# Two-layer block on one core: norms in blocks, gated attention outputs, a three-pass output projection, and a quarter of the gate rows on ScalarE

## The chip, the cores and the metric

One core of a Trainium2 chip runs the whole program in one launch. The metric is the device time of one execution in microseconds (us), as the median over runs. The engines are TensorE (PE, with its weight loads shown apart as PEld), VectorE (DVE), ScalarE (ACT), GpSimd (POOL) and SyncE (SP), which issues most DMAs. They run side by side and meet only at semaphores.

## The reference

The input is one sequence of 256 tokens with 1024 features, all in float32. Two layers follow each other. In layer 1, `h` goes through `rms_norm(h, g) * (1 + scale) + shift`, a projection, two mixers (a softmax attention and a recurrent mixer), a gated sum and `w_out`; then through a second norm and an expert layer, which for each token picks 8 x 16 of 16384 experts. In layer 2 the same kind of norm is followed by a projection, two attentions of 8 heads with 128 features (a: with three branches, b: with a compressed latent), and this:

```python
g_a, g_b = jnp.split(jax.nn.sigmoid(bgate), 2, axis=-1)
x = x + gate_a * ((g_a * o_a + g_b * o_b) @ w_o)
# rms_norm, scale and shift again, then a feed-forward with a short convolution:
# up (1024 -> 2 x 2816), conv, silu(gate) * up, down (2816 -> 1024), times gate_f, plus x
```

`scale`, `shift` and the gates of both layers come from one dot product for each feature between a conditioning vector and a row of `w_ada`.

## The kernel before

Everything is held transposed: 1024 features are 8 blocks of 128 partitions, 256 tokens lie along the free axis. The residual `hT` and the normed `xn` are 128x8x256. Weights come as 478 tiles of 128x1024 (512 KB) in one fixed order through `wring`, which has 6 slots; SyncE loads tile n when tile n - 6 is done (`tile_done`). Results go to three banks in turn, and the engine that empties one counts `ring_free`.

Products are made in two ways. Plain fp32 ones (`matmul8`, L438; `matmul8_tokens`, L488) take the weight slot as it is. Split ones (`three`, L463; `split8`, L470) take an upper part of the weight, rounded by ScalarE into one of three `whi` slots (`act_hi`, L450), and a rest that VectorE forms in `wlo` (`tile_lo`, L457), each against an upper and a lower part of x (`xhi`, `xlo`): three products for one. The phases in `SPLIT` are made this way; w_out and w_o are plain.

There is no planner: each engine has its program written out in order, and the order of the calls in the blocks at the end of the file is its queue. The phases that matter here:

- **Start.** VectorE does 16 dot products of `w_ada` (L822), the first norm, then 4 tiles of w_in by tokens (L492).
- **A norm** (four of them) is `norm_squares` (one VectorE operation over all 8 blocks, L514), `norm_pe` (8 products with ones, L506), `norm_act` (Sqrt, L511), `norm_scale` (reciprocal L518, one scaling over all blocks L519), `norm_shift` (8 operations, L523), `x_upper` on ScalarE (L530) and `x_rest` (L536). `pe_w_in` and `pe_w_in2` wait for all 8 blocks of `xn`, `pe_route` and `pe_ffn` for all of `xlo`. The two tiles after the second and fourth norm then need their own `act_hi` and `tile_lo`.
- **w_out** (L1422): VectorE adds each tile to `hT` (`dve_residual`, L1430) and does dot products of `w_ada` beside it (`dve_late_ada`, L1419; `dots_before` says how many by tile).
- **Routing and gate rows.** After the top-16 search on VectorE, the gates of 256 tokens are spread to a 128x128 table each, in 64 groups of 4 tokens: VectorE makes `A4` (one comparison over 512 columns, L1589) and `B4` (four operations of 128 columns, one a token, L1591), TensorE multiplies them (L1606) and does one eighth of an early expert tile (L1496), ScalarE copies the bank into the table `G` (L1616). `A4` and `B4` have two buffers, the banks four. After each eighth group ScalarE has a Gelu (L1505).
- **Expert stage** (256 tiles), then transposes, the residual (L1794) and the third norm.
- **Second attention** (`att_pe`, `att_act`, `att_dve`, `att_pool`, L575 to L687): 24 jobs for attention a and 8 for b, as a software pipeline in turns; in turn t VectorE finds the maxima of job t + 3, the reciprocals of job t + 1 and copies the output bank of job t - 2 (L674). GpSimd scales the probabilities (L686). After the last one VectorE multiplies `oA` and `oB` by their gates and adds them, three operations of 2048 columns (L2091 to L2093), and w_o starts (L2189).
- **Feed-forward** (66 tiles, split), at its end 8 additions into `hT` (L1803) and one store of 1 MB (L2323).

## Time and profile before

| | |
|---|---|
| median of 3 runs | 1910.35 us (1909.63 to 1910.8) |
| profiled execution | 1909.39 us |
| its span, first to last instruction | 1907.6 us |
| mean granted TensorE clock | 0.962 of full |
| busy: PE, PEld, DVE, ACT, POOL | 1731.3, 1503.9, 1337.7, 728.6, 98.9 us |
| HBM read, written | 309.63 MB, 5.51 MB |

Busy times are sums over one profiled execution; engines overlap, so they don't add up to the span. A TensorE that is shown busy may still be below its pace, since matmuls are pipelined and their ends are modelled. A row of a timeline gives the start, the busy time, the engine, the line of the code, the operation, what is written and read, the shape and the count; in brackets stands the idle time before it and what ended it.

### The profile page before, as it was taken

To read this page: it belongs to the slowest core of one execution; us is meant where nothing else is said; L and a number is where in the kernel's file an instruction comes from. 1 tells how busy PE (TensorE), PEld (TensorE's weight loads), DVE (VectorE), ACT (ScalarE), POOL (GpSimd) and SP (SyncE) were. 2 spreads that over 40 slices of the span, in tenths; PEclk is the share of its full clock that TensorE was granted. 3 is DMA by queue.
4 is the path that set the end of the run, shared out by engine and by line. 5 is a ranking of instruction groups with operands and counts; after the bars stand their busy time and mean duration, and the time that the engine had idled before them with its cause. 6 is when DMAs were issued, how large, how long until landed. Compare 5 with 4: busy or idle time off the path is not lost.

```text
span 1907.6 us, 30181 instructions
## 1 busy us (share of the span) xinstructions
PE 1731.3 (91%) x10370; PEld 1503.9 (79%) x10370; DVE 1337.7 (70%) x2720; ACT 728.6 (38%) x1275; POOL 98.9 (5%) x107
## 2 busy tenths in 40 slices
PE   2987999969997989999999999999799988879997
PEld 2986888759885767788888888887798846669997
DVE  7678553763999977688888888887445545448886
ACT  1443101113212344455555555554244215324443
POOL 0022000000000000000000000000007103200000
PEclk8999999989998989999999999999899988989999
DMA  9642003655561127677777777777355460035553
GB/s 332 233 136 69 23 16 108 216 216 165 159 189 46 56 81 242 211 234 240 233 237 235 236 239 234 239 234 222 110 181 152 125 209 1 23 96 180 182 181 110
DMA packets 101311, 316.24 MB, mean 166 GB/s; under 512 B 11248, under 2 KB 20464, under 8 KB 100720
## 3 DMA queue, kind: packets, MB, share of 16 engines
q1 hardware_dynamic: 100512, 311.07, 51.2%
q10 hardware_dynamic: 720, 4.11, 0.6%
q8 instruction: 50, 0.82, 0.2%
q14 instruction: 29, 0.24, 0.0%
HBM read 309.63 MB, written 5.51 MB: 165 GB/s over the span
## 4 chain that ended last, share of the span: by engine, by line
PE 77%; DVE 17%; DMA 2%; issue 2%; POOL 1%; ACT 1%; SPq 0%; ACTq 0%; DVEq 0%; POOLq 0%
PE bank L481 8%; PE bank L466 7%; PE bank L467 7%; PE bank L468 7%; PE bank L1647 6%; PE bank L1649 6%; PE bank L1651 6%; PE bank L482 4%; PE bank L1606 4%; PE bank L442 3%; PE bank L492 2%; PE bank L1398 2%; PE bank L582 1%; PE bank L1496 1%; PE bank L485 1%
## 5 line engine op out<-in xcount | busy, mean ns | idle before, releaser
L460 DVE TENSOR_TENSOR wlo<-wring,whi 128x1024 fp32r<-128x1024 f32 x348 | 423.9, 1224 | 114.5 <-ACT whi L455 106.7
L455 ACT CAST whi<-wring 128x1024 fp32r<-128x1024 f32 x364 | 380.9, 1048 | 73.5 <-PE bank L1651 49.1
L466 PE MATMUL bank<-xboth,whi 128*128 128x256 f32 x960 | 276.3, 288 | 25.5 <-DVE wlo L460 23.3
L467 PE MATMUL bank<-xboth,whi 128*128 128x256 f32 x960 | 273.3, 285 | 0.0
L468 PE MATMUL bank<-xboth,wlo 128*128 128x256 f32 x960 | 273.2, 285 | 0.0
L481 PE MATMUL bank<-xboth,whi 128*128 128x512 f32 x658 | 235.8, 397 | 0.0
L466 PEld LDWEIGHTS bank<-xboth,whi 128*128 128x128 f32 x960 | 186.0, 194 | 28.9 <-issue 24.4
L467 PEld LDWEIGHTS bank<-xboth,whi 128*128 128x128 f32 x960 | 186.1, 194 | 0.6 <-issue 0.5
L468 PEld LDWEIGHTS bank<-xboth,wlo 128*128 128x128 f32 x960 | 185.9, 194 | 0.0
L482 PE MATMUL bank<-xboth,wlo 128*128 128x256 f32 x658 | 184.5, 280 | 0.0
L1647 PE MATMUL bank<-whi,Whi 128*128 128x512 f32 x512 | 161.0, 396 | 14.9 <-DVE Wlo L1742 14.9
L1649 PE MATMUL bank<-wlo,Whi 128*128 128x512 f32 x512 | 159.9, 394 | 0.0
L1651 PE MATMUL bank<-whi,Wlo 128*128 128x512 f32 x512 | 159.0, 392 | 0.0
L481 PEld LDWEIGHTS bank<-xboth,whi 128*128 128x128 f32 x658 | 123.6, 188 | 29.4
L1496 PE MATMUL bank<-xn,wring 128*128 128x256 f32 x544 | 128.6, 380 | 0.0
L482 PEld LDWEIGHTS bank<-xboth,wlo 128*128 128x128 f32 x658 | 124.2, 189 | 3.7
L1647 PEld LDWEIGHTS bank<-whi,Whi 128*128 128x128 f32 x512 | 97.3, 191 | 33.4 <-issue 9.8
L1649 PEld LDWEIGHTS bank<-wlo,Whi 128*128 128x128 f32 x512 | 97.2, 190 | 21.5
L1651 PEld LDWEIGHTS bank<-whi,Wlo 128*128 128x128 f32 x512 | 97.0, 189 | 21.4
L1496 PEld LDWEIGHTS bank<-xn,wring 128*128 128x128 f32 x544 | 98.6, 191 | 10.7
L1751 DVE TENSOR_TENSOR arena<-arena 128x256 f32<-128x256 f32 x94 | 59.8, 636 | 56.0 <-ACT arena L1710 56.0
L460 POOL TENSOR_TENSOR wlo<-wring,whi 128x1024 fp32r<-128x1024 f32 x16 | 45.7, 2862 | 1016.4 <-ACT whi L455 1016.4
(367 smaller groups left out, 2893.5 us busy)
## 6 DMA issues: line engine op xcount, KB each, us to landing
wring<-in_w SPq DMA_DIRECT2D x463, 512.0 KB, 3.9
arena<-in_ada SPq DMA_DIRECT2D x48, 512.0 KB, 5.6
xn<-in_ada SPq DMA_DIRECT2D x96, 256.0 KB, 3.3
h_spill<-arena SPq DMA_DIRECT2D x34, 128.0 KB, 1.7
arena<-h_spill SPq DMA_DIRECT2D x34, 128.0 KB, 3.5
wring<-in_w SPq DMA_DIRECT2D x6, 384.0 KB, 3.1
wring<-in_w SPq DMA_DIRECT2D x9, 256.0 KB, 2.6
arena<-in_const ACTq DMA_DIRECT2D x1, 1200.0 KB, 5.3
```

Of the source, the lines that this page charges most:

```text
L455: act.copy(whi[:, n % HSLOTS, :], wring[:, n % SLOTS, :]).then_inc(hi_ready, 1)
L460: eng.tensor_tensor(wlo[:, n % SLOTS, :], wring[:, n % SLOTS, :], whi[:, n % HSLOTS, :].bitcast(F32), ALU.subtract).then_inc(lo_ready, 1)
L466: pe.matmul(out, h, xh, start=start, stop=False, **kw)
L467: pe.matmul(out, h, xl, start=False, stop=False, **kw)
L468: return pe.matmul(out, l, xh, start=False, stop=stop, **kw)
L481: pe.matmul(out, h, xboth[:, k, :, :], start=(k == 0), stop=False)
L482: pe.matmul(out[:, 0:S], l, xhi[:, k, :], start=False, stop=False)
L1496: mm = pe.matmul(bank[j % 3][:, 0:S], blocks(n % SLOTS, k), xn[:, k, :], start=(k == 0), stop=(k == KT - 1))
L1606: mm = pe.matmul(bank[3 + n % 4][:, t * 128:(t + 1) * 128], A4[:, n % 2, t, :], B4[:, n % 2, t, :], start=True, stop=True)
L1647: pe.matmul(tok_accs[b][f][:, :], Wh, h[:, f * 512:(f + 1) * 512], start=first, stop=False)
L1649: pe.matmul(tok_accs[b][f][:, :], Wh, l[:, f * 512:(f + 1) * 512], start=False, stop=False)
L1651: mm = pe.matmul(tok_accs[b][f][:, :], Wl, h[:, f * 512:(f + 1) * 512], start=False, stop=last)
```

## The change

- **Norms in blocks.** The squares go to ScalarE, one block at a time, behind the residual of that block (`act_square`); the sums with ones stand between the tiles of w_out and w_o, two tiles behind (`norm_sum`, in bank 4); the scaling is 8 operations on VectorE, and the shift moves to ScalarE (`norm_shift`), before or between the casts to the upper part. The first tile behind a norm waits for one block at a time.
- **First pair of tiles.** In wq and the feed-forward the first two tiles are done together, block by block, as pairs of `xlo` come (`split_pair`). Their upper and lower parts are made earlier, in the last tiles of w_out and w_o. For that `crow` (the conditioning vector) has another place, and the late dot products are spread otherwise over w_out's tiles (`DOTS`), none beside the last.
- **Second attention.** Outputs are multiplied by their gate in the operation that empties the bank. Attention a and b are added head by head, two turns or so behind, and the sum is split into `xhi` and `xlo`. w_o's first three tiles are split before and beside the last heads. Buffers of layer 2 lie elsewhere, so that `xboth` and `whi` are free.
- **w_o** is a split phase of three passes.
- **Gate rows.** VectorE makes three rows of `B4` a group. The fourth is made by ScalarE as Relu(gate - gate * (index - iota)^2), two operations (`act_hot`), two groups ahead; TensorE waits for both. A negated gate is made once (`ngate`).
- **End.** The last additions follow pairs of the last tile's blocks, and the store is four DMAs.
- Several semaphores of the head norms are merged into one each; their waits stay the same.

In the main blocks `norm_pe` goes from TensorE's order, `act_w_out` and `act_w_o` come into ScalarE's, and VectorE's `norm_scale` and `norm_shift` become `norm_root` and `norm_scale`. The core of the diff:

```diff
-SPLIT = ["w_in", "wq", "peer", "w_in2", "ffn"]
+SPLIT = ["w_in", "wq", "peer", "w_in2", "w_o", "ffn"]
...
-        def norm_pe(pe, n, sq):
-            pe.wait_ge(sq_ready, n + 1)
-            for k in range(KT):
-                mm = pe.matmul(bank[3][:, 0:S], ones, sq[:, k, :], start=(k == 0), stop=(k == KT - 1))
-            mm.then_inc(ss_ready, 1)
+        x_scaled = sem("x_scaled")
+        NORM_BANK = 4
+        def act_square(act, n, m, sq):
+            act.activation(sq[:, m, :], hT[:, m, :], ACT.Square).then_inc(sq_ready, 1)
+        def norm_sum(pe, n, m, sq):
+            pe.wait_ge(sq_ready, KT * n + m + 1)
+            mm = pe.matmul(bank[NORM_BANK][:, 0:S], ones, sq[:, m, :], start=(m == 0), stop=(m == KT - 1))
+            if m == KT - 1:
+                mm.then_inc(ss_ready, 1)
         def norm_act(act, n, rt):
             act.wait_ge(ss_ready, n + 1)
-            act.activation(rt, bank[3][:, 0:S], ACT.Sqrt, scale=1.0 / D, bias=col("eps")).then_inc(rt_ready, 1)
-        def norm_squares(dve, sq):
-            dve.tensor_tensor(sq[:, :, :], hT[:, :, :], hT[:, :, :], ALU.mult).then_inc(sq_ready, 1)
-        def norm_scale(dve, v, n, rt):
+            act.activation(rt, bank[NORM_BANK][:, 0:S], ACT.Sqrt, scale=1.0 / D, bias=col("eps")).then_inc(rt_ready, 1)
+        def norm_root(dve, v, n, rt):
             dve.wait_ge(rt_ready, n + 1)
             v.then(dve.reciprocal(rt, rt))
-            v.then(dve.tensor_tensor(xn[:, :, :], hT[:, :, :], over(rt, KT), ALU.mult))
-        def norm_shift(dve, n, shift):
+        def norm_scale(dve, rt):
             for k in range(KT):
-                dve.tensor_scalar(xn[:, k, :], xn[:, k, :], gsc[:, n, k:k + 1], modc(shift, k),
-                                  ALU.mult, ALU.add).then_inc(xn_ready, 1)
-        def x_upper(act, n):
+                dve.tensor_tensor(xn[:, k, :], hT[:, k, :], rt, ALU.mult).then_inc(x_scaled, 1)
+        def norm_shift(act, n, k, shift):
+            act.wait_ge(x_scaled, KT * n + k + 1)
+            act.activation(xn[:, k, :], xn[:, k, :], ACT.Identity, scale=gsc[:, n, k:k + 1],
+                           bias=modc(shift, k)).then_inc(xn_ready, 1)
+        def x_upper(act, n, k):
+            act.wait_ge(xn_ready, KT * n + k + 1)
+            act.copy(xhi[:, k, :], xn[:, k, :]).then_inc(x_hi, 1)
+        def norm_shift_split(act, n, shift):
+            norm_shift(act, n, 0, shift)
+            for k in range(1, KT):
+                norm_shift(act, n, k, shift)
+                x_upper(act, n, k - 1)
+            x_upper(act, n, KT - 1)
+        def norm_shift_plain(act, n, shift):
             for k in range(KT):
-                act.wait_ge(xn_ready, KT * n + k + 1)
-                act.copy(xhi[:, k, :], xn[:, k, :]).then_inc(x_hi, 1)
+                norm_shift(act, n, k, shift)
+            for k in range(KT):
+                x_upper(act, n, k)
+        def x_rest_pair(eng, n, k):
+            eng.wait_ge(x_hi, KT * n + k + 2)
+            eng.tensor_tensor(xlo[:, k:k + 2, :], xn[:, k:k + 2, :], xboth[:, k:k + 2, 0, :].bitcast(F32),
+                              ALU.subtract).then_inc(x_lo, 1)
         def x_rest(eng, n):
             for k in range(0, KT, 2):
-                eng.wait_ge(x_hi, KT * n + k + 2)
-                eng.tensor_tensor(xlo[:, k:k + 2, :], xn[:, k:k + 2, :], xboth[:, k:k + 2, 0, :].bitcast(F32),
-                                  ALU.subtract).then_inc(x_lo, 1)
+                x_rest_pair(eng, n, k)
+        def split_pair(pe, outs, n, norm):
+            for k in range(KT):
+                if k % 2 == 0:
+                    pe.wait_ge(x_lo, 4 * norm + k // 2 + 1)
+                for i in range(2):
+                    mm = three(pe, outs[i], n + i, k, xhi[:, k, :], xlo[:, k, :], k == 0 and (i == 0 or outs[2]),
+                               k == KT - 1, skip_group_check=True)
+                    if k == KT - 1:
+                        mm.then_inc(tile_done, 1)
...
+        def act_mix_upper(act, h):
+            act.wait_ge(mix_ready, h + 1)
+            act.copy(xhi[:, h, :], oA[:, h, :]).then_inc(mix_hi, 1)
+        def dve_mix(dve, h):
+            dve.wait_ge(a_free, MH + NH + h + 1)
+            dve.tensor_tensor(oA[:, h, :], oA[:, h, :], oB[:, h, :], ALU.add).then_inc(mix_ready, 1)
+        def dve_mix_rest(dve, h):
+            dve.wait_ge(mix_hi, h + 1)
+            dve.tensor_tensor(xlo[:, h, :], oA[:, h, :], xhi[:, h, :].bitcast(F32), ALU.subtract).then_inc(mix_lo, 1)
...
-                    dve.tensor_copy(j["out"], value_bank(j)[j["rows"], 0:S]).then_inc(a_free, 1)
+                    if j["weight"] is None:
+                        dve.tensor_copy(j["out"], value_bank(j)[j["rows"], 0:S]).then_inc(a_free, 1)
+                    else:
+                        dve.tensor_tensor(j["out"], value_bank(j)[j["rows"], 0:S], j["weight"], ALU.mult).then_inc(a_free, 1)
...
-        dots_before = lambda j: min(max(3 * j // 2, 0), 3 * KT)
+        DOTS = (0, 1, 3, 4, 6, 7, 9, 10, 12, 13, 15, 17, 19, 21, 23, 24, 24)
+        dots_before = lambda j: DOTS[min(max(j, 0), 2 * KT)]
...
+                       after=lambda k: k >= 2 and norm_sum(pe, 1, k - 2, nsq[1]))
+            for m in (KT - 2, KT - 1):
+                norm_sum(pe, 1, m, nsq[1])
+        def act_w_out(act):
+            w = FIRST["wq"]
+            for m in range(KT):
+                act.wait_ge(ring_free, RING0["w_out"] + m + 1)
+                act_square(act, 1, m, nsq[1])
+                if m in (5, 6):
+                    act_hi(act, w + m - 5, count_at(w + m - 5), None)
...
-            pe.wait_ge(x_lo, 8)
-            ring_tiles_split(pe, "wq")
+            w, r = FIRST["wq"], RING0["wq"]
+            pe.wait_ge(lo_ready, nth_split[w + 1])
+            pe.wait_ge(ring_free, r + 1 - BANKS + 1)
+            split_pair(pe, (bank[r % BANKS][:, 0:S], bank[(r + 1) % BANKS][:, 0:S], True), w, 1)
+            ring_tiles_split(pe, "wq", 2)
...
+            v.then(dve.tensor_copy(T3[:, 2, :], bank[4][:, 0:S]))
+            dve.tensor_scalar(rG["ngate"], T3[:, 2, :], -1.0, None, ALU.mult).then_inc(t3_ready, 1)
...
-                for t in range(4):
+                for t in range(3):
...
+        def act_hot(act, n):
+            t, away = 4 * n + 3, rG["away"][:, (n % 2) * 128:(n % 2) * 128 + 128]
+            if n >= 2:
+                act.wait_ge(hot_act, n - 1)
+            act.activation(away, rG["iota"], ACT.Square, scale=-1.0, bias=T3[:, 1, t:t + 1]).then_inc(away_ready, 1)
+            act.wait_ge(away_ready, n + 1)
+            act.activation(B4[:, n % 2, 3, :], away, ACT.Relu, scale=rG["ngate"][:, t:t + 1],
+                           bias=T3[:, 2, t:t + 1]).then_inc(hot_act, 1)
         def act_gates(act):
+            act.wait_ge(t3_ready, 1)
+            act_hot(act, 0)
+            act_hot(act, 1)
             for n in range(GROUPS):
                 act.wait_ge(g_ready, n + 1)
                 act.copy(G[:, 4 * n:4 * n + 4, :], bank[3 + n % 4][:, :].rearrange("p (t j) -> p t j", t=4))\
                    .then_inc(g_copied, 1)
+                if n + 2 < GROUPS:
+                    act_hot(act, n + 2)
...
+                if last and m % 2:
+                    mm.then_inc(acc_done, 1)
...
-                ins = dve.scalar_tensor_tensor(hT[:, m, :], accs[m], modc(vec, m), hT[:, m, :], ALU.mult, ALU.add)
-            ins.then_inc(acc_read, 1)
-            dve.wait_ge(acc_read, 2)
+                if m % 2 == 0:
+                    dve.wait_ge(acc_done, m // 2 + 1)
+                dve.scalar_tensor_tensor(hT[:, m, :], accs[m], modc(vec, m), hT[:, m, :], ALU.mult,
+                                         ALU.add).then_inc(acc_read, 1)
...
+            def beside(t):
+                h = t - 3 * NH - 3
+                if 0 <= h:
+                    dve_mix(dve, h)
+                if 0 <= h - 2:
+                    dve_mix_rest(dve, h - 2)
+                if 0 <= h and h < 3:
+                    tile_lo(dve, FIRST["w_o"] + h, nth_split[FIRST["w_o"] + h])
+            att_dve(dve, v, nsa_jobs + mla_jobs, beside=beside)
+            for h in range(MLH - 1, MLH):
+                dve_mix(dve, h)
+            for h in range(MLH - 3, MLH):
+                dve_mix_rest(dve, h)
...
+            for t in range(HSLOTS):
+                act_hi(act, FIRST["w_o"] + t, count_at(FIRST["w_o"] + t), None)
+            att_act(act, nsa_jobs + mla_jobs, beside=lambda t: t >= 3 * NH + 4 and act_mix_upper(act, t - 3 * NH - 4))
+            for h in range(MLH - 2, MLH):
+                act_mix_upper(act, h)
...
-            pe.wait_ge(mix_ready, 1)
-            ring_tiles(pe, "w_o", lambda slot, bk: matmul8(pe, bk[:, 0:S], slot, oA))
+            first, ring0 = FIRST["w_o"], RING0["w_o"]
+            for t in range(KT):
+                n = first + t
+                pe.wait_ge(lo_ready, nth_split[n])
+                pe.wait_ge(ring_free, ring0 + t - BANKS + 1)
+                for k in range(KT):
+                    if t == 0:
+                        pe.wait_ge(mix_lo, k + 1)
+                    mm = three(pe, bank[(ring0 + t) % BANKS][:, 0:S], n, k, xhi[:, k, :], xlo[:, k, :], k == 0, k == KT - 1)
+                mm.then_inc(tile_done, 1)
+                if t >= 2:
+                    norm_sum(pe, 3, t - 2, nsq[3])
+            for m in (KT - 2, KT - 1):
+                norm_sum(pe, 3, m, nsq[3])
+        def act_w_o(act):
+            for m in range(KT):
+                act.wait_ge(ring_free, RING0["w_o"] + m + 1)
+                n = FIRST["w_o"] + HSLOTS + m
+                if m < KT - 1:
+                    act_hi(act, n, count_at(n), None)
+                act_square(act, 3, m, nsq[3])
...
-            sp.wait_ge(acc_read, 2)
-            sp.dma_start(a["out"], hT[:, :, :]).then_inc(stored, 16)
-            sp.wait_ge(stored, 16)
+            for m in range(0, KT, 2):
+                sp.wait_ge(acc_read, KT + m + 2)
+                sp.dma_start(a["out"][:, m:m + 2, :], hT[:, m:m + 2, :]).then_inc(stored, 16)
+            sp.wait_ge(stored, 16 * (KT // 2))
```

## Rows read from the trace of the kernel before

**Rows 1.** The page, part 4: the chain that ended last, shares of the span.

```profile
PE 77%; DVE 17%; DMA 2%; issue 2%; POOL 1%; ACT 1%; SPq 0%; ACTq 0%; DVEq 0%; POOLq 0%
```

**Rows 2.** Timeline, norm after w_out: start us, busy us, engine, line, operation, tiles, count.

```profile
407.75 0.48 DVE L1430 SCALAR_TENSOR_TENSOR hT<-bank,mod,hT 128x256 f32<-128x256 f32 x1 [1.83 <-PE bank L442]
419.31 1.75 DVE L518 RECIPROCAL arena<-arena 128x256 f32<-128x256 f32 x1 [6.29 <-ACT arena L511]
429.78 0.58 PE L466 MATMUL bank<-xboth,whi 128*128 128x256 f32 x1 [11.08 <-DVE wlo L460]
```

**Rows 3.** Timeline around the norm after the expert stage.

```profile
1333.47 3.23 DVE L1794 SCALAR_TENSOR_TENSOR hT<-bank,mod,hT 128x256 f32<-128x256 f32 x8 [0.75 <-PE bank L1687]
1344.90 1.75 DVE L518 RECIPROCAL arena<-arena 128x256 f32<-128x256 f32 x1 [5.88 <-ACT arena L511]
1351.75 1.65 PE L492 MATMUL bank<-wring,xn 128*128 128x128 f32 x6 [7.39 <-DVE xn L523]
```

**Rows 4.** Timeline from the end of the second attention to the feed-forward.

```profile
1648.56 0.42 DVE L674 COPY arena<-bank 128x256 f32<-128x256 f32 x1 [0.41 <-PE bank L611]
...
1692.83 1.75 DVE L518 RECIPROCAL arena<-arena 128x256 f32<-128x256 f32 x1 [4.32 <-ACT arena L511]
...
1703.32 0.55 PE L466 MATMUL bank<-xboth,whi 128*128 128x256 f32 x1 [11.04 <-DVE wlo L460]
```

**Rows 5.** The chain of waits in order of time: start us, us, what.

```profile
433.98 0.21 PE bank L466
435.26 0.12 PE bank L466
...
643.66 0.43 PE bank L1496 x2
```

**Rows 6.** Groups of ScalarE instructions by shape: count, busy us, mean ns, idle before.

```profile
L626 ACT ACTIVATE arena<-arena 128x128 f32<-128x128 f32 x32 | 12.9, 403 | 2.2 <-DVE arena L657 1.6
L530 ACT CAST xboth<-xn 128x256 fp32r<-128x256 f32 x32 | 10.7, 405 | 29.1 <-DVE xn L523 29.1
```

**Rows 7.** Timeline of one group of gate rows (in brackets: idle before, releaser).

```profile
598.40 0.69 DVE L1589 TENSOR_TENSOR arena<-arena 128x512 f32<-128x512 f32 x1
598.55 0.97 PEld L1606 LDWEIGHTS bank<-arena 128*128 128x128 f32 x8 [0.44 <-DVE arena L1591]
599.00 1.11 DVE L1591 TENSOR_SCALAR arena<-arena 128x128 f32<-128x128 f32 x4
599.43 0.30 PEld L1496 LDWEIGHTS bank<-xn,wring 128*128 128x128 f32 x2
599.74 0.59 ACT L1616 COPY arena<-bank 128x512 f32<-128x512 f32 x1 [1.04 <-PE bank L1606]
```

**Rows 8.** The chain of waits, all of the span, at w_o.

```profile
1655.89 29.78 PE bank L442 x128
```

**Rows 9.** Six turns of attention: stretch, length, busy us of PE, PEld, DVE, ACT, POOL.

```profile
1629.50:1643.30 13.80, 13.80 (x91) 12.55 (x90) 6.52 (x40) 8.57 (x30) 5.05 (x12) 1.00 0.01 2
```

**Rows 10.** Timeline of the start.

```profile
33.37 1.23 DVE L822 CUSTOM_DVE_ANT_0 arena<-arena 128x1024 f32<-128x1024 f32 x1
41.22 16.45 PE L492 MATMUL bank<-wring,xn 128*128 128x128 f32 x128 [18.06 <-DVE xn L523]
```

**Rows 11.** The DMAs of line 725 (w_in's first tiles), issue to landing.

```profile
L725 SPq DMA_DIRECT2D wring<-in_w x6: 431/606/821, 29.7 to 32.9; - x6
DMA to landing us min/median/max: 6.3/8.3/9.6
```

**Rows 12.** Timeline of the end.

```profile
1900.01 3.23 DVE L1803 SCALAR_TENSOR_TENSOR hT<-bank,mod,hT 128x256 f32<-128x256 f32 x8 [4.69 <-PE bank L468]
1903.26 0.35 SPq L2323 DMA_DIRECT2D out_hT<-hT  x1
```

**Rows 13.** Timeline of ScalarE before the second attention.

```profile
1568.30 0.47 ACT L2179 ACTIVATE arena<-bank,cols 128x256 f32<-128x256 f32 x1 [3.92 <-PE bank L2130]
1568.79 1.28 ACT L626 ACT_TABLE_LOAD   x1
```

249 lines of the change are left out of this document (130 added, 119 removed).

## The prediction, made before the changed kernel was built or run

> **What bounds the kernel now.** I read the page's chain of waits first, then the chain in order of time, and then the timeline of each place where the chain leaves TensorE. The chain is on TensorE for 77% of the span and on VectorE for 17% [rows 1]. The long streams (the expert stage, the second input projection, the feed-forward) are TensorE at full pace, and the change doesn't alter them. What it alters is six places that the chain crosses one after the other, so a microsecond gained in one is a microsecond of the span, unless something outside the six is late: the start, the first gate-and-norm seam (after w_out), the 64 groups of gate rows, the norm after the expert stage, the second attention with w_o and the norm behind it, and the end. In the seams TensorE waits for whole-tensor steps of VectorE: from the last w_out residual at 407.75 us to the first wq product at 429.78 is 22.0 us [rows 2], from the expert stage's residual at 1333.47 to 1351.75 is 18.3 us [rows 3], from the last attention copy at 1648.56 over w_o to the first feed-forward product at 1703.32 is 54.8 us [rows 4].
>
> **Prices used.** One 128x128 by 256-column three-pass product is spaced 0.12 us at the full clock and 0.21 us at the half one, and a plain fp32 one of 256 columns takes 0.43 us as its two halves [rows 5]. After a seam about 20 products run at the half clock: the first ones after 429.78 are 0.21 us apart and by 435.26 they are at 0.12 [rows 2, 5]. A square, a shift or a copy of 256 columns on ScalarE: the trace has no Identity with two column operands and no Square, so I bound them by the cast's 0.33 us from start to start (2.67 us for 8; its mean of one is 0.405) and by 0.6 us, and take 0.45 [rows 6]. A 256-column VectorE step is 0.42 us, 0.33 from start to start.
>
> **Norm after w_out.** Removed from the path: the squares in one piece (2.3), 8 sums (5.9), the scaling in one piece (2.3), and the wait for all of x. Added: the sums of tiles 0 to 4 stand in TensorE's order ahead of the last w_out tile, 5 x 0.43 = 2.2 us later, at 409.9; then residual 0.5, last square 0.45, last sum 0.6, root 0.5, reciprocal 1.76. The Sqrt table is now loaded behind the squares: 1.28 us, of which about 0.8 is beyond the sum that runs beside it. VectorE's queue (bias, gains, one lower tile: 1.7 us) ends just about then. The reciprocal ends near 414.4 instead of 421.06 [rows 2]: 6.7 us. From there: the old way needed 8.7 us to the first product, then 20 x 0.21 + 28 x 0.12 = 7.6 us for two tiles, so 16.3. The new way feeds pairs of blocks at ScalarE's rate, 0.45 + 0.33 = 0.8 us a block. The first pair is there after 2.9 us, TensorE at the half clock is slower than that, so 2.9 + 7.6 = 10.6. Gain 5.7, together **12.4 us** (8 if the clock stays half for both tiles, 14 if it never falls). The moved dot products of the modulation (2 of 1.15 us a tile beside 3.9 us of TensorE) are hidden; if their DMAs were late the residuals would wait, 0 to 2 us.
>
> **Norm after the expert stage.** The squares follow the eight residuals at 0.4 us each, the last ends at 1337.2. The constants' DMA issue and the table load follow on ScalarE's queue (0.35 + 1.28), root 0.5 and reciprocal 1.8 end at 1341.1 instead of 1346.7 [rows 3]. One block scaled and shifted is 1.0 us against the whole tensor's 5.1. **9.7 us** (7 to 11).
>
> **Gate rows.** A group takes 1.63 us now, and VectorE has no gap in it: the comparison of 512 columns starts 0.60 us before the four row steps, which take the remaining 1.02, 0.255 each [rows 7]. TensorE's weight loads sit idle 0.44 us of each group for VectorE [rows 7], so it can do about 1.3 a group (8 loads of a group, 0.89, and 0.43 beside them), though the chain of waits, with modelled ends, shows it as always busy. With three row steps VectorE needs 1.37. ScalarE gets a Square and a Relu of 128 columns for each group, between copies of 0.59 us, and has 1.04 us idle [rows 7]. The nearest row is the 128-column activation with a column operand, 0.403 us [rows 6]; the Relu has two operands and waits for the Square. I take 0.49 (the copy, start to start) + 0.43 + 0.49 less 0.09 of overlap = 1.32, plus the Gelu of each eighth group, 0.04: 1.36. Loop over two groups: TensorE 1.2 + ScalarE 1.45 = 2.65, so 1.33. Three engines at 1.3 to 1.37 with two buffers hinder each other a little, I take 1.42. (1.628 - 1.42) x 62 = 12.9, less 0.4 for the negated gate: **12.6 us** (between 16 at 1.37 and 0 if TensorE really is the bound).
> The Trainium skill ("ScalarE: Activation LUTs", Rules for kernel authors) says that relu and multiply belong on VectorE. The rows agree that the step is dearer there (about 0.9 against 0.255 us); it pays only because ScalarE waits 1.04 us a group. By the same page (What ACT_TABLE_LOAD costs) each pointer operand adds 93 ns; with that the sum stays the same within 0.1 us a group.
>
> **Attention, w_o and its norm.** The three gating steps after attention, 2.3 us each in the 7.3 us between 1648.56 and w_o's first product at 1655.89 [rows 4, 8], go: the gate is applied in the step that empties the bank, at the same 0.42 us. But VectorE gets, for each of the last heads, an addition and a subtraction (0.33 each), and for three heads a lower tile (1.15). In the last steady jobs it is busy 6.52 of 13.8 us for six jobs, 1.1 of 2.3 [rows 9]; with about 1.9 more in three turns these turns take 2.9 to 3.1. The reciprocals of the last two heads stand behind them in VectorE's order, and GpSimd, the transposes and the values wait for those. So attention ends about 2.7 us later, and the last block's upper and lower parts come at 1654; TensorE has most of tile 0 done by then. w_o starts in effect at 1651.6 instead of 1655.9. Its eight tiles are 8 x 24 x 0.12 = 23.0 us instead of 29.8 [rows 8], plus 2.2 for five sums, plus 1 for a part at the half clock (the old first tile lost 2.2 to it): 1677.8 against 1685.7. Then residual, square, sum, table, root, reciprocal 4.9: 1682.6 against 1694.6 [rows 4], 12.0 us. The first pair of the feed-forward as above: 5.7. Together **17.7 us** (12 to 22). Split work for w_o (upper 1.05, lower 1.22, square 0.45) fits beside 3.3 us of TensorE a tile.
>
> **Start.** The dot products are held by DMA until 28.1 us, so squares are free. The four last ones start at 33.37 behind the scaling [rows 10]; without it they start at 31.05, but the last weight's DMA was issued late and I let it end at 35.7. Then one block instead of eight: first product at 37.1, not 41.22. The w_in tile lands 6.3 us or more after 29.75 [rows 11], at 36.1 or later, so this can be a microsecond less. **4.1 us** (2 to 5).
>
> **End.** The last additions are 3.23 us after the last product, then one 1 MB store takes from 1903.26 to the span's end, 4.3 us [rows 12]. New: two additions (0.8) after the last product and a store of a quarter; a 256 KB transfer isn't free, I take 2.8. **4.0 us** (2 to 5).
>
> **Sum.** 4.1 + 12.4 + 12.6 + 9.7 + 17.7 + 4.0 = 60.5 us. The profiled execution took 1909.4 (span 1907.6 and 1.8 around it), 1 us under the median of 1910.35. 1909.4 - 60.5 = 1848.9. I predict **1849 us**.
>
> **A rule on tables.** In the trace a table load costs 1.28 us and starts 0.02 us after the activation before it [rows 13]. The Trainium skill (same page, What ACT_TABLE_LOAD costs) adds a drain of about 1.38 us to each switch; the trace shows none. By the page the three exposed Sqrt loads would cost 4 us more, 1853. The page (Table sets: the hidden batching unit) names relu, copy and identity as members of every set, and Square only in a list of accuracies.
>
> **Rivals.**
> A, Square or Relu isn't in the set that Gelu uses. Then each of the eight Gelus inside the gate groups brings two loads: 8 x 2.57 = 20.5 us on ScalarE, which has no slack left; the norms lose up to 1 us each. 1849 + 22 = 1871. For it: the trace has neither function. Against: copies and casts never cause a load. Chance 0.08.
> B, the gate groups don't get faster: TensorE at 1.59 us (1.16 + 0.43 in the chain), or ScalarE at 1.6. 1849 + 12.6 = 1862. For it: the chain's modelled ends. Against: idle weight loads. Chance 0.12.
> C, the seams give back half: TensorE, fed in small pieces, stays at the half clock through the pairs and into w_o, and the pairs wait for ScalarE at 0.93 us a block. Two pairs lose 4 each, w_o 3, the norm sums 2: 1862. Chance 0.12.
> D, slower than before: Square and Relu live in different sets, so that every group has two loads between them. ScalarE's group would be 1.36 + 2.57 = 3.9 us, 64 x 2.3 = 147 us longer, while the other places save 48: 1909 + 99 = 2008. It decides from 0.75 us lost a group on (48 / 64). Chance 0.03.
>
> **Numbers.** Forecast 0.65 (1842 to 1857). The range 1839 to 1866 takes in B and C and leaves A and D out. A measurement tells 0.2% (3.8 us) from no change; only D or an unseen cause reaches that: faster 0.95, same 0.02, slower 0.03.
>
> **What would show it.** Groups of gate rows 1.37 to 1.45 us apart, with three VectorE row steps and the idle time of TensorE's loads near 0.2; one table load for each norm, none among the gate groups; reciprocal to first product below 3.2 us at wq and the feed-forward, two tiles done 10 to 11 us after it; w_o's tiles about 3.3 us apart, the value products of the last head 2 to 3 us later than now relative to the attention's start; first product by 38 us. The forecast is wrong if the groups stay at 1.6, if loads stand among them, or if what the early stages gain is missing at the start of the expert stage (about 29 us earlier than 704.9).

## The result and the profile after

Over four runs each on one chip, the changed kernel took 1848.28 us (median; 1846.67 to 1850.49) and the kernel before 1910.57 us (1909.63 to 1912.66). The ratio is 0.967, with a 95% interval of 0.966 to 0.969: faster, by 62.3 us. The forecast was 1849, so the total is right; the parts are less exactly right, as the table shows (stretches in us). The profiled execution has a span of 1844.9 us instead of 1907.6, which is 62.7 us to divide up. I cut both traces at the same events and compared the stretches between them. There is one trace of the kernel before, and each trace has TensorE at its half clock in places of its own, so a gain of the table is that of this pair of traces.

| stretch (from event to event) | before | after | gain | forecast |
|---|---|---|---|---|
| start to the first w_in product | 41.22 | 37.32 | 3.9 | 4.1 |
| to w_out's first product | 338.60 | 339.88 | -1.3 | 0 |
| to the copy of wq's second tile | 58.01 | 46.28 | 11.7 | 12.4 |
| to the first comparison of the gate rows | 151.09 | 150.55 | 0.5 | 0 |
| to the first expert product | 116.03 | 100.64 | 15.4 | 12.6 |
| to the first residual of the expert stage | 628.52 | 629.01 | -0.5 | 0 |
| to w_in2's first product | 18.29 | 8.56 | 9.7 | 9.7 |
| to the second attention's first product | 227.24 | 224.80 | 2.4 | 0 |
| to the end of the norm's reciprocal | 115.58 | 103.37 | 12.2 | 12.0 |
| to the copy after the feed-forward's fourth tile | 22.36 | 17.63 | 4.7 | 5.7 |
| to the copy after its last pair of tiles | 173.49 | 173.75 | -0.3 | 0 |
| to the end of the last addition | 12.81 | 10.37 | 2.4 | 2.4 |
| to the end of the span | 4.33 | 2.72 | 1.6 | 1.5 |

The copy of wq's second tile, where the third stretch ends, comes 0.9 us behind the tile's last product: ScalarE has a cast of 1.05 us between the copies of the first two tiles. So 0.9 us of the gain of the norm after w_out stands in the stretch behind it.

The first product, against [rows 10]:

```profile
37.32 0.98 PE L498 MATMUL bank<-wring,xn 128*128 128x128 f32 x3 [16.38 <-ACT xn L535]
```

The page after, part 4, against [rows 1]: the share on VectorE fell from 17 to 15%, TensorE's rose to 78%, and DMAs have 3%, half of it (28 us) at the start, where VectorE waits for the rows of `w_ada`.

```profile
PE 78%; DVE 15%; DMA 3%; POOL 2%; issue 2%; ACT 1%; SPq 0%; DVEq 0%; ACTq 0%; POOLq 0%
```

Timeline of the norm after w_out, against [rows 2] (start us, busy us, engine, line, operation, tiles, count, idle before and what ended it).

```profile
407.29 0.48 DVE L1496 SCALAR_TENSOR_TENSOR hT<-bank,mod,hT 128x256 f32<-128x256 f32 x1 [1.12 <-PE bank L446]
407.81 0.42 ACT L513 ACTIVATE arena<-hT 128x256 f32<-128x256 f32 x1 [2.54 <-DVE hT L1496]
408.25 1.28 ACT L523 ACT_TABLE_LOAD   x1
409.54 0.47 ACT L523 ACTIVATE arena<-bank,cols 128x256 f32<-128x256 f32 x1
410.05 1.75 DVE L527 RECIPROCAL arena<-arena 128x256 f32<-128x256 f32 x1 [0.59 <-ACT arena L523]
411.83 2.77 DVE L531 TENSOR_TENSOR xn<-hT,arena 128x256 f32<-128x256 f32 x8
414.09 0.39 ACT L541 CAST xboth<-xn 128x256 fp32r<-128x256 f32 x1
414.52 0.69 DVE L561 TENSOR_TENSOR xboth<-xn,xboth 128x512 fp32r<-128x512 f32 x1
415.36 0.55 PE L470 MATMUL bank<-xboth,whi 128*128 128x256 f32 x1 [6.37 <-DVE xboth L561]
```

From the last residual to the first wq product is now 8.1 us, not 22.0. The reader should see two things here. The Sqrt waits for its table: the load ends at 409.53 and the Sqrt starts at 409.54. And the first difference, L561, for which TensorE waits, has two things ahead of it that end together: the eight scalings in VectorE's queue (411.83 to 414.60) and ScalarE's second cast (414.09 to 414.48). The same chain stands in front of the feed-forward: the reciprocal ends at 1640.40, the first product starts at 1643.97.

The norm after the expert stage, against [rows 3], has one scaling and one shift between the reciprocal and the first product:

```profile
1303.68 3.23 DVE L1887 SCALAR_TENSOR_TENSOR hT<-bank,mod,hT 128x256 f32<-128x256 f32 x8 [0.75 <-PE bank L1775]
1312.24 0.98 PE L498 MATMUL bank<-wring,xn 128*128 128x128 f32 x3 [3.83 <-ACT xn L535]
```

A group of gate rows, against [rows 7]. VectorE takes three row steps (0.86) and starts a group every 1.37 us; ScalarE has copy, Square and Relu back to back, with no idle time left. Each eighth group, where ScalarE has a Gelu too, takes 1.47 or 1.48 us, so that the mean over 48 groups is 1.385; the weight loads' idle time fell from 0.44 to 0.18.

```profile
619.60 0.59 ACT L1700 COPY arena<-bank 128x512 f32<-128x512 f32 x1
619.63 0.69 DVE L1658 TENSOR_TENSOR arena<-arena 128x512 f32<-128x512 f32 x1
620.08 0.41 ACT L1689 ACTIVATE arena<-arena 128x128 f32<-128x128 f32 x1
620.23 0.86 DVE L1660 TENSOR_SCALAR arena<-arena 128x128 f32<-128x128 f32 x3
620.52 0.49 ACT L1691 ACTIVATE arena<-arena 128x128 f32<-128x128 f32 x1
620.97 0.59 ACT L1700 COPY arena<-bank 128x512 f32<-128x512 f32 x1
621.00 0.69 DVE L1658 TENSOR_TENSOR arena<-arena 128x512 f32<-128x512 f32 x1
621.14 0.97 PEld L1676 LDWEIGHTS bank<-arena 128*128 128x128 f32 x8 [0.18 <-DVE arena L1660]
```

The end of the second attention and w_o, against [rows 4, 8]. The last output leaves its bank at 1610.46; behind it stand only two additions and the differences, and w_o, already running since 1609.90, ends with the residual at 1635.90. Its residuals are 3.30 us apart.

```profile
1610.46 0.42 DVE L733 TENSOR_TENSOR arena<-bank,arena 128x256 f32<-128x256 f32 x1
1611.80 1.09 DVE L699 TENSOR_TENSOR xboth<-arena,xboth 128x256 fp32r<-128x256 f32 x3
1635.90 0.48 DVE L1496 SCALAR_TENSOR_TENSOR hT<-bank,mod,hT 128x256 f32<-128x256 f32 x1 [2.82 <-PE bank L472]
```

The end, against [rows 12]: two additions behind the last product, and four stores whose last quarter ends the span.

```profile
1841.28 0.88 DVE L1899 SCALAR_TENSOR_TENSOR hT<-bank,mod,hT 128x256 f32<-128x256 f32 x2 [0.40 <-PE bank L472]
1838.72 3.80 SPq L2451 DMA_DIRECT2D out_hT<-hT  x4
```

### The profile page after: what moved, and what is told of

The parts are those of the page before. It is cut to its first block, busy times and chain, and to the rows that moved or that the text cites. A ratio compares the mean times of both kernels' runs of the same rounds, so it can differ in the third digit from the quotient of the medians.

```text
span 1844.9 us, 30479 instructions
## 1 busy us (share of the span) xinstructions
PE 1706.8 (93%) x10434; PEld 1498.2 (81%) x10434; DVE 1312.5 (71%) x2670; ACT 808.0 (44%) x1483; POOL 101.0 (5%) x107
## 4 chain that ended last, share of the span: by engine, by line
PE 78%; DVE 15%; DMA 3%; POOL 2%; issue 2%; ACT 1%; SPq 0%; DVEq 0%; ACTq 0%; POOLq 0%
PE bank L485 8%; PE bank L470 7%; PE bank L471 7%; PE bank L472 7%; PE bank L1735 6%; PE bank L1737 6%; PE bank L1739 6%; PE bank L486 4%; PE bank L1676 3%; PE bank L498 2%; PE bank L1453 2%; DMA arena<-in_ada 2%; PE bank L446 2%; PE bank L1564 2%; PE bank L621 1%
## 5 line engine op out<-in xcount | busy, mean ns | idle before, releaser
L464 DVE TENSOR_TENSOR wlo<-wring,whi 128x1024 fp32r<-128x1024 f32 x356 | 433.9, 1224 | 109.8 <-ACT whi L459 100.6
L459 ACT CAST whi<-wring 128x1024 fp32r<-128x1024 f32 x372 | 388.6, 1046 | 78.2 <-PE bank L1739 49.4
L470 PE MATMUL bank<-xboth,whi 128*128 128x256 f32 x1024 | 295.0, 288 | 16.2 <-DVE xboth L561 12.8
L471 PE MATMUL bank<-xboth,whi 128*128 128x256 f32 x1024 | 290.8, 284 | 0.0
L472 PE MATMUL bank<-xboth,wlo 128*128 128x256 f32 x1024 | 290.7, 284 | 0.0
L470 PEld LDWEIGHTS bank<-xboth,whi 128*128 128x128 f32 x1024 | 197.6, 193 | 20.1 <-issue 15.1
L471 PEld LDWEIGHTS bank<-xboth,whi 128*128 128x128 f32 x1024 | 197.7, 193 | 0.7 <-issue 0.5
L472 PEld LDWEIGHTS bank<-xboth,wlo 128*128 128x128 f32 x1024 | 197.5, 193 | 0.0
L486 PE MATMUL bank<-xboth,wlo 128*128 128x256 f32 x658 | 184.5, 280 | 0.0
L1735 PE MATMUL bank<-whi,Whi 128*128 128x512 f32 x512 | 161.2, 396 | 15.5 <-DVE Wlo L1835 15.5
L485 PEld LDWEIGHTS bank<-xboth,whi 128*128 128x128 f32 x658 | 123.6, 188 | 29.4
L486 PEld LDWEIGHTS bank<-xboth,wlo 128*128 128x128 f32 x658 | 124.2, 189 | 3.7
```

The lines of the kernel that those rows point to most:

```text
L459: act.copy(whi[:, n % HSLOTS, :], wring[:, n % SLOTS, :]).then_inc(hi_ready, 1)
L464: eng.tensor_tensor(wlo[:, n % SLOTS, :], wring[:, n % SLOTS, :], whi[:, n % HSLOTS, :].bitcast(F32), ALU.subtract).then_inc(lo_ready, 1)
L470: pe.matmul(out, h, xh, start=start, stop=False, **kw)
L471: pe.matmul(out, h, xl, start=False, stop=False, **kw)
L472: return pe.matmul(out, l, xh, start=False, stop=stop, **kw)
L485: pe.matmul(out, h, xboth[:, k, :, :], start=(k == 0), stop=False)
```

## Experiments

All kernels here are built from the changed one. The time of one kernel spread over up to 15.5 us on these chips (the kernel before: 1900.9 to 1916.4 in 11 runs beside the last four), so differences of a few microseconds are read from the stretches of the table above; those that don't contain a fall of TensorE's clock repeat within 0.3 us from one trace to the next. Where a stretch does contain one, the trace to compare with is one that has the fall in the same place; "from the reciprocal" counts from the end of the norm's reciprocal.

**1. The gate row back on VectorE**

```diff
-                for t in range(3):
+                for t in range(4):
                     ins = dve.tensor_scalar(B4[:, b, t, :], ...
...
-                pe.wait_ge(hot_act, n + 1)
...
-            act_hot(act, 0)
-            act_hot(act, 1)
...
-                if n + 2 < GROUPS:
-                    act_hot(act, n + 2)
```

> The changed kernel with the fourth gate row of each group back on VectorE; all else stays. What the gate rows bring, alone. In the changed kernel the 64 groups are 1.37 us apart and the first expert product comes at 674.7 us, after a start of the gate groups at about 574. Theory (VectorE's four row steps set the group): groups 1.63 us apart again, VectorE without a gap, first expert product at 690 us, time +15 to +16 us (1863 to 1865) and none of it lost or regained later. Rival 1 (the prediction's own figure, that three engines hinder each other at 1.42): +12.6 us, 1861. Rival 2 (part of the gain in the gates comes from TensorE's clock or from the early products, not from the row): groups between 1.45 and 1.6, +5 to +10 us.

Measured: 1865.44 us (1856.71 to 1868.55), the kernel before beside it 1912.45, ratio 0.974 (0.971 to 0.976). The groups are 1.63 us apart again, VectorE without a gap:

```profile
621.18 0.68 DVE L1658 TENSOR_TENSOR arena<-arena 128x512 f32<-128x512 f32 x1
621.78 1.10 DVE L1660 TENSOR_SCALAR arena<-arena 128x128 f32<-128x128 f32 x4
622.81 0.68 DVE L1658 TENSOR_TENSOR arena<-arena 128x512 f32<-128x512 f32 x1
```

From the first comparison to the first expert product it took 116.59 us instead of 100.64. The theory of the group holds: the row alone is worth 15.9 us in that stretch. The 12.6 of the prediction (rival 1) was too low. The span of this trace is 21.9 us longer, though, not 15.9: 5.7 us more stand in the expert stage (634.7 us instead of 629.0), which the edit doesn't touch and which took 625.4 to 631.6 in the other eleven experiments. What lengthened it isn't shown.

**2 to 4. What sets the 1.37 us of a group**

```diff
+            dve.memset(B4[:, :, 2, :], 0.0)
...
-                for t in range(3):
+                for t in range(2):
...
-            act.activation(away, rG["iota"], ACT.Square, scale=-1.0, bias=T3[:, 1, t:t + 1]).then_inc(away_ready, 1)
-            act.wait_ge(away_ready, n + 1)
+            if n < 2:
+                act.activation(away, rG["iota"], ACT.Square, scale=-1.0, bias=T3[:, 1, t:t + 1]).then_inc(away_ready, 1)
+                act.wait_ge(away_ready, n + 1)
```

The first edit leaves VectorE's third row out (it stays zero), the second leaves the Square out after the second group (the Relu reads an old distance), and the last kernel has both.

> The changed kernel with one of VectorE's three row steps left out of every group (that row of B4 is zero, so a quarter of the gate table is left out of the result); ScalarE and TensorE keep their work. It asks which engine sets the 1.37 us of a group. Theory (VectorE and ScalarE are level: copy 0.48 + Square 0.44 + Relu 0.47 from start to start is 1.39): groups stay at 1.36 to 1.40, VectorE gets 0.25 us of idle time a group, time within 2 us of the changed kernel. Rival 1 (VectorE alone sets it): 1.2 to 1.3 a group, 5 to 10 us faster. Rival 2 (TensorE sets it): nothing moves in this and in the next two runs.

> The changed kernel with the Square on ScalarE done for the first two groups only, so that each later group's Relu reads an old distance (that row of the gate table is wrong from group 2 on); VectorE keeps three row steps. ScalarE's group falls from 1.39 to about 0.95 us. Theory (VectorE and ScalarE level): groups stay at 1.36 to 1.38, VectorE without a gap, time within 2 us of the changed kernel. Rival 1 (ScalarE alone sets it): 1.2 to 1.3 a group, 5 to 10 us faster. Rival 2 (TensorE sets it): nothing moves.

> Both of the last two edits together: two row steps on VectorE (1.12 us a group with the comparison), only a copy and a Relu on ScalarE (0.95), the gate table wrong in the same rows. It shows TensorE's own floor. Theory (VectorE and ScalarE level at 1.37, TensorE close behind): groups at 1.2 to 1.3 us, 4 to 10 us faster than the changed kernel, and TensorE's weight loads without idle time. Rival (TensorE at 1.37): no move at all. If it falls to 1.12 TensorE's floor lies below VectorE's and my estimate of about 1.3 from eight loads of 0.89 and 0.43 beside them was too high.

Measured between one comparison and the next: 1.33 and 1.35 in turn, with 1.57 where a Gelu falls, 1.366 on the mean, with the row left out; 1.372 without the Square, the same where a Gelu falls; 1.325 with neither; and 1.385 in the changed kernel (means over 48 groups). (Times: 1844.96, 1846.24 and 1845.38 us, two runs each, 1841.3 to 1848.6 in all, too few and too wide to tell 3 us.) The three kernels in this order, one group each:

```profile
620.57 0.58 ACT L1701 COPY arena<-bank 128x512 f32<-128x512 f32 x1
621.48 0.49 ACT L1692 ACTIVATE arena<-arena 128x128 f32<-128x128 f32 x1
621.92 0.58 ACT L1701 COPY arena<-bank 128x512 f32<-128x512 f32 x1
```

```profile
620.11 0.59 ACT L1701 COPY arena<-bank 128x512 f32<-128x512 f32 x1 [0.40 <-PE bank L1676]
620.13 0.70 DVE L1658 TENSOR_TENSOR arena<-arena 128x512 f32<-128x512 f32 x1
621.50 0.70 DVE L1658 TENSOR_TENSOR arena<-arena 128x512 f32<-128x512 f32 x1
```

```profile
620.76 1.08 PEld L1677 LDWEIGHTS bank<-arena 128*128 128x128 f32 x8
621.76 0.30 PEld L1564 LDWEIGHTS bank<-xn,wring 128*128 128x128 f32 x2
622.09 0.19 PEld L1677 LDWEIGHTS bank<-arena 128*128 128x128 f32 x1
```

With the row out ScalarE is full (1.35 from copy to copy). Without the Square VectorE is full, and ScalarE has 0.40 idle. With neither it is the weight loads that stand end to end: ten in 1.33 us. So the theory holds: VectorE needs 1.372 us a group, ScalarE 1.366 and TensorE 1.325. Together they take 1.385, since a group with a Gelu is 0.1 us late and nothing makes up for it: 0.013 x 62 = 0.8 us is all that they cost each other. Moving more work would gain about 3 us: with neither step the stretch to the first expert product is 97.31 us, 3.3 less than in the changed kernel.

**5. w_o as plain fp32 products**

```diff
-SPLIT = ["w_in", "wq", "peer", "w_in2", "w_o", "ffn"]
+SPLIT = ["w_in", "wq", "peer", "w_in2", "ffn"]
...
-                    mm = three(pe, bank[(ring0 + t) % BANKS][:, 0:S], n, k, xhi[:, k, :], xlo[:, k, :], ...
+                    mm = pe.matmul(bank[(ring0 + t) % BANKS][:, 0:S], blocks(n % SLOTS, k), oA[:, k, :], ...
```

(and without the sum's upper parts and differences and w_o's upper and lower tiles)

> The changed kernel with w_o as plain fp32 products again (8 of 0.43 us a tile instead of 24 of 0.12): no lower tiles and no upper and lower parts of the attention's sum on VectorE and ScalarE; the gating at the bank's exit, the squares and sums of the norm and all else stay. In the changed kernel the last attention copy is at 1610.46, w_o's first product at 1609.9, its last residual at 1635.90. Theory (the split moves 3.8 us into the attention's last turns, where VectorE has eight differences and three lower tiles more, and gives 0.57 us a tile back): attention ends 3 to 3.5 us sooner, w_o takes 27.5 to 29.8 instead of 23, residual 1 to 3.5 us later, time +1 to +3.5 us. Rival 1 (the split is worth its whole 6.8 us and the tail is late for another reason): +5 to +7 us. Rival 2 (the split loses): faster than the changed kernel.

Measured: 1842.88 us (1840.1 to 1848.01), the kernel before beside it 1912.19. By stretches:

```profile
1607.45 0.42 DVE L733 TENSOR_TENSOR arena<-bank,arena 128x256 f32<-128x256 f32 x1
1637.24 0.48 DVE L1496 SCALAR_TENSOR_TENSOR hT<-bank,mod,hT 128x256 f32<-128x256 f32 x1 [3.40 <-PE bank L2292]
```

From the attention's first product to its last output 69.83 us (with the split 73.42), from there to the last residual 29.79 (25.44). Tiles are 3.45 us apart without a sum between (2.87 with the split). Together plain is 0.8 us longer, and against the changed kernel's second trace (71.98 and 25.45, below) 2.2. The trace that is like this one in TensorE's clock, at the attention's start and in its last turns, is that of the kernel without the Square: 72.92 and 25.45, so that plain is 1.2 us longer, at the low end of the theory. Rival 1 (6.8) is out. The whole time doesn't show the split to be worth anything: the ratio to the kernel before is 0.964 (0.961 to 0.967) here and 0.967 (0.966 to 0.969) and 0.966 (0.964 to 0.968) in the two measurements of the changed kernel. And from last output to last residual the kernel before took 37.13: the 7.3 us that are missing in the plain version are exactly the gating steps between 1648.56 and 1655.89 [rows 4, 8]. The gate at the bank's exit brings the gain of this place, the three passes one or two microseconds by the stretches.

**6. The norm's sums behind the tiles**

```diff
-            ring_tiles(pe, "w_out", ..., after=lambda k: k >= 2 and norm_sum(pe, 1, k - 2, nsq[1]))
-            for m in (KT - 2, KT - 1):
+            ring_tiles(pe, "w_out", ...)
+            for m in range(KT):
                 norm_sum(pe, 1, m, nsq[1])
```

(the same in w_o)

> The changed kernel with the norm's eight sums behind the last tile of w_out and of w_o instead of between the tiles. Theory (the gain of these seams comes from the squares made beside the tiles, not from where the sums stand): each product stage ends six sums of 0.43 us, 2.6 us, sooner; six sums then run while the last residual, square and the table load pass, and the Sqrt starts at the later of load and sum, about 1.2 us sooner than now: 409.54 becomes 408.3 and 1638.15 becomes 1636.9. Time 2 to 3 us faster in all. Rival (sums between the tiles save what they take): the eight sums stand on the path again, 2 to 4 us slower.

Measured: 1843.32 us (1839.38 to 1847.5). w_out's first product to the reciprocal's end: 33.64 us, with sums between the tiles 34.60. Last output to reciprocal: 29.07 instead of 29.95.

```profile
399.77 3.62 PE L517 MATMUL bank<-arena,keep 128*128 128x256 f32 x16
400.92 1.28 ACT L523 ACT_TABLE_LOAD   x1
403.42 0.47 ACT L523 ACTIVATE arena<-bank,cols 128x256 f32<-128x256 f32 x1 [1.22 <-PE bank L517]
```

The table load lies beside the eight sums, and the Sqrt waits for the last of them. 1.0 and 0.9 us a seam are won up to the reciprocal, 1.2 were expected: the rival is wrong, and the place of the sums was no part of the change's gain. Behind the reciprocal part of it goes again, since the half clock begins later there: the copy of wq's second tile comes 12.29 us after it instead of 11.68, and that of the feed-forward's fourth tile 18.76 instead of 18.37 (the changed kernel's second trace), which leaves 0.35 and 0.5. What remains for the gain up to the reciprocal are the squares beside the tiles and, after w_out, the two dot products of `w_ada` (2.3 us) that no longer stand behind the last residual; no run takes these away alone.

**7. Two tiles one after the other**

```diff
-            for k in range(KT):
-                if k % 2 == 0:
+            for i in range(2):
+                for k in range(KT):
+                    if i == 0 and k % 2 == 0:
                         pe.wait_ge(x_lo, ...)
-                for i in range(2):
```

> The changed kernel with the first two tiles of wq and of the feed-forward taken one after the other; the first tile still waits for its blocks of x one pair at a time. Theory (x in blocks brings most of the gain, the pair order only fills TensorE while ScalarE feeds 0.8 us a block): the first tile ends 8.0 to 8.5 us after the reciprocal, the second at 11.2 to 12 instead of 10.4, so +0.8 to +1.5 us in the seam of wq. At the feed-forward the first tile frees its slot sooner, the upper part of the fourth tile and the convolution come 1.5 us sooner, which takes the loss back: 0 there. Time +0.5 to +2.5 us. Rival (the pair order is what brings the 5.7 us of each seam): +6 to +11 us.

Measured: 1848.36 us (1846.79 to 1851.39). From the reciprocal to the copy of wq's first tile 9.6 us and of its second 12.62; at the feed-forward the copy comes after 12.04 and the next 5.70 later, 17.74 in all. Against the changed kernel's first trace (11.68 and 17.63) that is 0.9 and 0.1 us more. But there TensorE left the half clock sooner: in the 13 us behind wq's reciprocal the granted clock was 0.75, here 0.62. Three traces have the pair order and the clock of this one (experiments 1, 3 and 4); here are experiment 1 and then this kernel, 13 us from the reciprocal on:

```profile
411.90:424.90 13.00, 9.40 (x56) 9.44 (x57) 6.72 (x14) 8.46 (x19) 1.49 (x2) 0.62 0.26 84
```

```profile
410.20:423.20 13.00, 9.43 (x53) 9.05 (x54) 7.92 (x15) 9.11 (x21) 1.49 (x2) 0.62 0.37 121
```

In those three the second tile's last product ends 12.26 us after the reciprocal, here 12.59, and the third tile's copy comes at 15.16 to 15.19 instead of 15.50: the pair order is worth 0.3 us at wq. At the feed-forward the traces whose half clock lies where it does here (the changed kernel's second, experiments 1, 2 and 4) have the first two copies at 12.30 to 12.34 and 18.37 to 18.41, here 12.03 and 17.74, and the copy after the last pair at 192.12 to 192.16, here 191.22. So there the pair order costs 0.9 us, 0.6 of them behind the pair, and over both seams it loses 0.6. The rival is wrong, and the theory right only in that the order matters little. What the seams gain comes from x in blocks and from the weight parts made earlier, which no run takes apart.

**8. w_o's lower tiles six turns sooner**

```diff
-                if 0 <= h and h < 3:
-                    tile_lo(dve, FIRST["w_o"] + h, nth_split[FIRST["w_o"] + h])
+                if -6 <= h and h < -3:
+                    tile_lo(dve, FIRST["w_o"] + h + 6, nth_split[FIRST["w_o"] + h + 6])
```

> The changed kernel with the three lower tiles of w_o made on VectorE six turns sooner, in the turns where it has 1.37 us idle, instead of in the turns of the last heads, where the additions and differences stand too. Theory (VectorE's order in the last turns delays the reciprocals, GpSimd and the transposes by 3.8 us): the last attention copy comes 2.5 to 3.5 us sooner than 1610.46, w_o as much sooner, time 2.5 to 3.5 us faster. Rival (the eight additions and differences alone, or ScalarE's casts, hold the tail): less than 1 us.

Measured: 1842.45 us (1839.32 to 1846.73), and the theory is wrong. First product to last output: 72.61 us. The changed kernel's 73.42 isn't its equal, since TensorE's clock stood otherwise at the attention's start (last section). Of the kernels that started like it, the one without the Square took 72.92, also without a fall of the clock in its last turns, and the one with a gate row left out 73.11, with a short one. So 0.3 us were gained, as the rival said. The idle time that I filled wasn't spare:

```profile
1587.76 0.29 DVE L709 CUSTOM_DVE_ANT_0 arena<-bank,arena 128x128 f32<-128x128 f32 x1
1589.13 1.29 DVE L464 TENSOR_TENSOR wlo<-wring,whi 128x1024 fp32r<-128x1024 f32 x1
1591.29 0.29 DVE L709 CUSTOM_DVE_ANT_0 arena<-bank,arena 128x128 f32<-128x128 f32 x1 [0.88 <-PE bank L621]
```

In that turn the next maxima start 0.9 us late (3.53 us after the one before, 2.62 without the lower tile), and two turns on 0.8 us late: by VectorE's order the step delays the reciprocal that GpSimd and the transposes wait for, and the maxima then wait 0.88 us for TensorE. The output copy behind these turns comes at 59.59 us of the attention instead of 57.57 (without the Square); the last turns make up for it.

**9 to 12. Again, one store, repairs, all together**

```diff
+            act.activation(out[:, 0:1], col("eps"), ACT.Sqrt).then_inc(table, 1)
...
-            norm_shift(act, n, 0, shift)
-            for k in range(1, KT):
-                norm_shift(act, n, k, shift)
-                x_upper(act, n, k - 1)
-            x_upper(act, n, KT - 1)
+            for k in range(0, KT, 2):
+                norm_shift(act, n, k, shift)
+                norm_shift(act, n, k + 1, shift)
+                x_upper(act, n, k)
+                x_upper(act, n, k + 1)
...
-            for n in range(F0 + 2, F0 + 4):
-                hi(n, 0)
+            hi(F0 + 2, 0)
             act.wait_ge(pad_ready, 1)
-            turn(0)
+            z(0, 0)
+            hi(F0 + 3, 0)
+            silu(0, 0)
```

(the repairs: the first line loads the table ahead of the last square, the second part is ScalarE's order on x, the third the feed-forward's first turn, where VectorE also makes the fourth tile's lower part later; one store has a single `dma_start` of the whole output behind the last addition, and the last kernel has the repairs and the edits of experiments 6 and 8)

> The changed kernel itself, once more, beside the next three runs on the same chip. Expected: the first measurement again, 1848 us within 4 us, ratio 0.966 to 0.969. From the traces so far I expect its stages to repeat within 0.3 us where the granted clock falls in the same places, and the rest of the spread to come from how long TensorE is held at the half clock (95 to 116 us in all in the runs so far).

> The changed kernel with one store of the whole output behind the last addition instead of four behind pairs of blocks. Theory (the prediction's term): the last addition ends at 1842.16 and the last quarter's store takes 2.7 us to the span's end; one store takes 4.3 us as in the kernel before, so the span ends 1.5 us later relative to the last addition. Rival (a store costs the same whatever its size): no difference within 0.3 us in that stretch.

> The changed kernel with three small repairs at its seams: a Sqrt of one column ahead of the last squares, so that the table is loaded while ScalarE waits for a tile; ScalarE's order on x as shift, shift, upper, upper; and in the feed-forward's first turn the copy of z ahead of the upper part of the fourth tile, with the lower part behind the first two steps of the convolution. Theory: the Sqrt follows the last sum (0.8 us sooner after w_out and after w_o, 0.25 after the expert stage); reciprocal to first product 3.0 instead of 3.5 us, two tiles done 0.3 to 0.5 us sooner each time; end of the first pair to the first down product 6.4 instead of 7.8 us. Together 4.0 us faster than the changed kernel. Rival 1 (Square isn't in the table with Sqrt): two loads a seam, 2.6 us slower in each of the two long seams. Rival 2 (TensorE's lead is used up by the wait for x at the half clock anyway): only the tables' 1.8 us.

> The last kernel's three repairs, with the norm's sums behind the last tile of w_out and w_o, and the three lower tiles of w_o six turns sooner. Theory, from the parts: 4.0 (seams) + 1.2 (with the table loaded ahead, sums behind the tiles gain 0.6 us a seam) + 2.4 (lower tiles: 61.5 us from the seventh maxima to the last attention copy became 59.0) = 7.6 us faster than the changed kernel beside it, 1840 to 1841 us, unless the granted clock takes it back. Rival (the gains overlap, or each is followed by as much time at the half clock): 2 to 4 us.

Measured, all on one chip beside a kernel before of 1910.02 us: the changed kernel 1844.91 (1841.57 to 1846.87, 6 runs; ratio 0.966, 0.964 to 0.968), one store 1845.46 (2 runs), the repairs 1844.2 (1841.97 to 1848.07, 4 runs), all together 1841.47 (1838.16 to 1844.83, 6 runs).

One store: from the last addition to the span's end 4.33 us, with four stores 2.74. The theory holds, 1.6 us. The store is issued at 1843.24, and the span ends at 1847.5:

```profile
1843.24 0.35 SPq L2450 DMA_DIRECT2D out_hT<-hT  x1
```

The repairs: of 4.0 us expected, little came.

```profile
406.15 1.28 ACT L515 ACT_TABLE_LOAD   x1
408.73 0.42 ACT L519 ACTIVATE arena<-hT 128x256 f32<-128x256 f32 x1 [1.08 <-DVE hT L1504]
409.93 0.47 ACT L529 ACTIVATE arena<-bank,cols 128x256 f32<-128x256 f32 x1 [0.79 <-PE bank L523]
414.92 0.68 DVE L567 TENSOR_TENSOR xboth<-xn,xboth 128x512 fp32r<-128x512 f32 x1
```

```profile
1655.09 0.39 PE L470 MATMUL bank<-Whi,whi 128*128 128x256 f32 x1 [1.41 <-DVE wlo L464]
```

The table is loaded in the wait for the last tile, the Square after it needs none (rival 1 is wrong), and residual to reciprocal's end is 4.04 instead of 4.51 us: 0.5 a seam, not 0.8, since the last sum itself ends only then. The new order on ScalarE brought nothing: its second cast now ends 2.2 us after the reciprocal instead of 2.7, but the first difference still starts behind the eight scalings, and reciprocal to first product is 3.55 us as before. I had read ScalarE as the one that feeds this place; in the changed kernel both reach it within 0.1 us, so either alone gains nothing. In the feed-forward the wait only moved: the first down product waits 1.41 us for its lower tile, against 1.66 in the changed kernel, but it comes 7.1 us after the end of the pair instead of 6.7 (6.4 were expected). VectorE has the same steps to do in whatever order.

All together: the changed kernel's median beside it less 3.4 us, a ratio of 0.9983 of the mean logarithms (0.9969 to 0.9997). It is faster than both kernels, by what the rival gave it. By stretches w_out to reciprocal is 33.64 (34.60), last output to reciprocal 29.05 (29.95), first product to last output as in experiment 8; with the sums behind the tiles the early table has nothing left to hide.

## Why the prediction was right, and where not

The mechanism of the six places was in the main the one that the traces show, and five of six terms are within 1.5 us. The sum is right partly because misses cancel: the gate rows gave 2.8 us more and the feed-forward's pair 1.0 less, and 2.4 us came from a stretch whose work is the same, against 1.3 lost between the start and w_out. One of the signs that were to show it failed: reciprocal to first product was to be below 3.2 us and is 3.55.

**Gate rows**: forecast 12.6, measured 15.4 (15.9 by experiment 1). The step that failed is "three engines at 1.3 to 1.37 with two buffers hinder each other a little, I take 1.42". VectorE's 1.37 was right to the hundredth, ScalarE's 1.36 nearly (1.366), TensorE's "about 1.3" is 1.325, and the groups are 1.385 us apart on the mean: the hindrance is 0.013 us a group (the Gelu's), not 0.05, and (1.42 - 1.385) x 62 = 2.2 us of the 2.8 that are missing. Rival B, for which the chain's modelled ends spoke, is refuted; the idle time of the weight loads [rows 7] was the better witness.

**Norm after w_out**: 12.4 against 11.7 in the table and 12.6 at the third tile: w_out's first product to the reciprocal's end took 34.60 us instead of 41.25, and from there to the third tile's copy 13.70 instead of 19.64. Part of this is not the norm's: in the kernel before two dot products of `w_ada` stood between the last residual and the squares (408.15 to 410.43), and the new `DOTS` moved them. The prediction's list of what goes leaves them out, though its sum, which adds the new path up afresh, has them in. Residual to reciprocal's end is 4.5 us as forecast; the first product comes 3.55 us behind the reciprocal where I took 2.9. The step counted two shifts and two casts at 0.45 and 0.33 us. A shift is 0.50 from start to start, a third one stands ahead of the second cast, and the difference stands in VectorE's order behind eight scalings too; both ways end 2.7 us after the reciprocal, and the difference and its product follow. That the pair is still done 10.8 us after the reciprocal (forecast 10.5) is luck of the clock: 13 of its products are 0.21 us apart, where I took 20. In three later traces of kernels that are the same up to here the half clock lasted 10.3 us instead of 6.8, the pair was done after 12.3, and the stretch of the table took 47.73 to 47.76 us instead of 46.28. The sums between the tiles, 2.2 us in my working, were costed as a necessity; they cost 1.0 us more than sums behind (experiment 6).

**Norm after the expert stage**: 9.7 and 9.7.

**Attention, w_o, norm**: to the reciprocal 12.0 forecast, 12.2 measured, but otherwise split. The attention ends 3.85 us later (forecast 2.7), 1.45 of it because TensorE, waiting in the last turns, fell to the half clock for longer: in the second trace of the same kernel it did so for half as long and needed 71.98 us (granted clock 0.66 and 0.83 in the two rows below, of the first and the second trace). Against that, the first eight outputs came 1.2 us sooner than in the kernel before (56.40 us after the first product, 57.58 before), by the clock at the attention's start (last section). The last turns by themselves cost 3.4 us where no fall lies in them (15.35 us from the eighth output to the last without the Square, 11.99 before), not 2.7. From the last output on 16.1 us are gained where I had 14.7.

```profile
1600.00:1610.00 10.00, 8.07 (x33) 6.95 (x34) 8.00 (x23) 4.32 (x13) 5.65 (x7) 0.66 0.00 1
```

```profile
1600.00:1610.00 10.00, 8.09 (x44) 7.09 (x44) 9.38 (x28) 4.96 (x15) 5.63 (x7) 0.83 0.00 1
```

The pair at the feed-forward: 5.7 forecast, 4.7 measured. The step left out that the fourth tile's upper part waits for a slot that the pair holds to its end, so that 1.05 us of ScalarE and 1.23 of VectorE come ahead of the convolution. Experiment 7, which frees that slot sooner, bears it out: behind the first copy it is 0.6 us ahead (0.4 in this stretch, 0.3 in the next). The rest of the miss stands ahead of the first copy (11.56 us after the reciprocal, 16.65 before, a gain of 5.1). In nine of the twelve later traces the half clock began later behind the reciprocal or lasted longer, and the stretch took 18.4 to 18.8 us, a gain of 3.6 to 4.0.

**Start**: 3.9 of 4.1 at the first product (which came at 36.1 to 37.9 us over the thirteen traces), but 1.3 us are given back by w_out. The first tile now starts before its blocks are there and takes 6.6 us to its copy instead of 5.8, which is 0.9 of them. The rest stays open: the same stretch took 338.9 to 340.6 us in nine later traces and 334.1 to 334.7 in three.

**End**: 2.4 + 1.6 = 4.0, forecast 4.0; the store's part confirmed by itself. That the sum comes out so exactly is luck of the traces: in both TensorE was at the half clock for 3.4 us close to its last products. In nine of the twelve later traces it wasn't, and the additions' stretch took 9.24 to 9.26 us instead of 10.37.

**The 2.4 us before the attention** can't be put down to the change: the work in that stretch is the same, and it comes in two forms, 224.7 to 225.2 us and 227.2 to 227.8, with the longer one in the kernel before and in three of the twelve experiments. With one trace of the kernel before it stays open whether it would show the shorter one as well.

Rivals A and D: there is no table load among the gate rows and one a norm. Square and Relu ran between Gelus without a load, Identity behind the Sqrt, and Square behind it too (the repairs). The Trainium skill ("ScalarE: Activation LUTs", Table sets: the hidden batching unit) lists relu and identity as part of every set; the trace agrees as far as it goes (Relu with Gelu's, Identity with Sqrt's), and shows Square with both. On its drain (same page, What ACT_TABLE_LOAD costs) the trace disagrees again: square's end to Sqrt is the load's 1.28 us and nothing more (408.25 to 409.54 above). Rival C: the half clock did follow the seams, but for 6.8 us, not through both tiles and w_o. It came nearer in other traces: 10.3 us behind the norm after w_out in four, 10.2 behind that after w_o in three.

## What to carry to other kernels

When work moves between engines inside a loop, add up each engine's start-to-start times and take the largest nearly as it is; with two buffers three engines at 1.372, 1.366 and 1.325 us ran at 1.385. Feed a product stage block by block and make its squares beside the tiles, but follow every way to the first block: eight scalings ahead of one difference took as long as the shifts and casts, and shortening one of the two gained nothing. Idle time inside a pipelined turn is not spare if a later engine waits for what follows it. And compare two stretches only where TensorE's clock stood alike in both: without that, the pair order looked 0.9 us better at the first seam, where it is worth 0.3, and level at the second, where it costs 0.9.

## What the hardware showed that I had not expected

The granted clock of TensorE differs between executions of the same work, and carries microseconds. Here are the same sixteen products of the first layer, in the changed kernel and in the one with the sums behind the tiles, where nothing ahead of them differs. Both wait 3.5 us for VectorE; in one they then run at the half level (1.2 GHz) and take 3.78 us, in the other at the full one (2.4 GHz) and take 2.05. w_out began at 377.2 us in one and 372.0 in the other. Of these 5.2 us, 1.0 stands ahead of the sixteen products, 2.5 come in and right behind them (both traces are then 3.5 us apart until 346 us), and 1.7 in a second stretch at the half clock, 346.5 to 349.9 us, which the other trace doesn't have.

```profile
221.33 3.78 PE L1356 MATMUL bank<-arena 128*128 128x128 f32 x16 [3.48 <-DVE arena L1228]
```

```profile
220.33 2.05 PE L1356 MATMUL bank<-arena 128*128 128x128 f32 x16 [3.47 <-DVE arena L1228]
```

The 16 us ahead of the second attention, in the changed kernel and in the version with everything together (stretch, length, busy us of PE, PEld, DVE, ACT, POOL, the granted clock, DMA share, GB/s):

```profile
1521.00:1537.00 16.00, 4.78 (x58) 2.81 (x55) 9.89 (x23) 6.37 (x8) 0.00 (x0) 0.81 0.23 78
```

```profile
1519.00:1535.00 16.00, 5.67 (x45) 3.04 (x45) 9.28 (x23) 4.87 (x6) 0.00 (x0) 0.52 0.11 34
```

With 0.81 of the full clock the stretch from w_in2 to the attention took 224.80 us, with 0.52 227.59, and the attention's first turns 1.4 us more as well. Over thirteen traces of these closely related kernels, TensorE stood at the half level (1.2 GHz) for 95 to 116 us in all, in the kernel before for 148. Behind the shortened seams the slow part was shorter in most of them, not in all: 6.8 or 10.3 us behind the norm after w_out (10.3 before), 3.4 behind the one after the expert stage (6.8 before). The expert stage, which no kernel here changed, took between 625.4 and 634.7 us.
